# Key tile ahead of the tile of values and gates, in each input quarter of a float32 encoder layer on one core

## The reference

```python
h = rms_norm(x, norm_mix)
proj = h @ w_in      # 2048 x 4624; columns: qa 1024, ka 256, va 256, qf, kf, vf 1024 each, f 16
qa, ka = rope(qa), rope(ka)
out_a = swa_sink_attention(qa, ka, va, sinks)        # 16 query heads, 4 key heads
log_f = log_sigmoid(f_logit + b_f)                   # 16 gates per token
out_b = forgetting_attention(qf, kf, vf, log_f)      # bias: cumulative sum of log_f
x = x + concat(out_a, out_b) @ w_o
h = rms_norm(x, norm_ffn)
x = x + conv_gated_ffn(h, w_up, conv_w, conv_b, w_down)
return rms_norm(x, norm_final)
```

## Time and profile before

| what | kernel before |
|---|---|
| median of 3 runs | 1062.1 us |
| the profiled execution, its own time | 1060.14 us |
| its span, first to last instruction | 1058.3 us |
| PE busy | 1048.7 us (99%) |
| DVE, ACT, POOL busy | 787.5, 626.9, 86.6 us |
| mean DMA rate over the span | 245 GB/s |
| mean granted TensorE clock | 0.998 |

### The profile page before, as it was taken

The page is one execution under the profiler, slowest core; times in us unless marked ns, Lnnn a source line. Parts: engine busy times, 40 slices in busy tenths (PEclk is TensorE's granted clock), DMA queues, the critical chain, the costliest instruction groups (busy, mean ns, idle before and its releaser), DMA issues.

```text
span 1058.3 us, 17826 instructions
## 1 busy us (share of the span) xinstructions
PE 1048.7 (99%) x5945; PEld 904.9 (86%) x5945; DVE 787.5 (74%) x1174; ACT 626.9 (59%) x971; POOL 86.6 (8%) x150
## 2 busy tenths in 40 slices
PE   9999999999999999999999999999999999999997
PEld 8888888888888888888888888888888888888885
DVE  5677677776555777777777877777877888877777
ACT  6956475756455555555655565555656666646663
POOL 1000000011111010111111010101111000000000
PEclk9999999999999999999999999999999999999999
DMA  9575656587888898998898898989889688887993
GB/s 300 173 231 161 186 169 176 168 256 202 246 252 231 263 250 276 253 270 235 256 275 249 267 237 272 268 256 262 249 259 258 224 294 293 274 298 266 322 316 107
DMA packets 191493, 259.35 MB, mean 245 GB/s; under 512 B 10820, under 2 KB 140580, under 8 KB 191328
## 3 DMA queue, kind: packets, MB, share of 16 engines
q1 hardware_dynamic: 173776, 215.32, 63.1%
q0 software_dynamic: 17360, 43.22, 18.7%
q10 hardware_dynamic: 320, 0.34, 0.1%
HBM read 256.73 MB, written 44.06 MB: 284 GB/s over the span
## 4 chain that ended last, share of the span: by engine, by line
PE 98%; DMA 1%; DVE 0%; SPq 0%; ACT 0%; issue 0%; DVEq 0%
PE tr_ps L1579 15%; PE pj L1579 15%; PE pj L1331 9%; PE pj L1581 8%; PE tr_ps L1581 8%; PE pj L1319 5%; PE pj L1320 5%; PE pj L1321 5%; PE pj L1333 5%; PE sc_ps L1319 4%; PE sc_ps L1321 4%; PE sc_ps L1320 4%; PE pj L1346 3%; PE pj L1348 1%; PE tr_ps L1320 1%; PE tr_ps L1321 1%
## 5 line engine op out<-in xcount | busy, mean ns | idle before, releaser
L889 DVE TENSOR_TENSOR split<-raw,split 128x1024 fp32r<-128x1024 f32 x266 | 321.7, 1223 | 146.7 <-ACT split L578 141.4
L578 ACT ACTIVATE split<-raw 128x1024 fp32r<-128x1024 f32 x260 | 270.7, 1057 | 97.2 <-PE pj L1581 28.7
L1579 PE MATMUL tr_ps<-act_split,split 128*128 128x512 f32 x704 | 245.5, 392 | 0.0
L1579 PE MATMUL pj<-act_split,split 128*128 128x512 f32 x704 | 245.0, 391 | 0.0
L1581 PE MATMUL pj<-act_split,split 128*128 128x256 f32 x704 | 197.6, 281 | 0.0
L1581 PE MATMUL tr_ps<-act_split,split 128*128 128x256 f32 x704 | 197.6, 281 | 0.0
L1168 DVE TENSOR_TENSOR split<-raw,split 128x1024 fp32r<-128x1024 f32 (+1 forms) x124 | 137.2, 1136 | 37.9 <-ACT split L834 35.7
L834 ACT ACTIVATE split<-raw 128x1024 fp32r<-128x1024 f32 (+1 forms) x124 | 119.5, 987 | 69.0 <-PE sc_ps L1321 31.9
L1579 PEld LDWEIGHTS tr_ps<-act_split,split 128*128 128x128 f32 x704 | 131.8, 187 | 28.5
L1579 PEld LDWEIGHTS pj<-act_split,split 128*128 128x128 f32 x704 | 131.7, 187 | 28.6
L1331 PE MATMUL pj<-act_split,split 128*128 128x512 f32 x416 | 147.1, 398 | 0.0
(11 more groups left out here) (240 smaller groups left out, 1512.6 us busy)
## 6 DMA issues: line engine op xcount, KB each, us to landing
raw<-w_up SPq DMA_DIRECT2D x176, 512.0 KB, 6.0
raw<-w_in SPq DMA_DIRECT2D x72, 512.0 KB, 3.8
raw<-w_down SPq DMA_DIRECT2D x68, 512.0 KB, 5.6
t_dram<-w_down POOLq DMA_DIRECT2D x60, 512.0 KB, 6.5
raw<-t_dram SPq DMA_DIRECT2D x40, 512.0 KB, 5.7
raw<-w_o SPq DMA_DIRECT2D x32, 512.0 KB, 5.7
t_dram<-t_dram POOLq DMA_DIRECT2D x40, 256.0 KB, 6.0
raw<-w_down SPq DMA_DIRECT2D x20, 256.0 KB, 5.6
```

Of the source, the lines that this page charges most:

```text
L578: ins = act.activation(hi[:, slot, 0:TILE], raw[:, slot, 0:TILE], ACT.Copy)
L889: dve.tensor_tensor(lo[:, slot, 0:n], raw[:, slot, 0:n], hi[:, slot, 0:n].bitcast(F32), ALU.subtract).then_inc(lo_done, 1)
L1579: pe.matmul(up_banks[v][b], wh[:, c, b * P:(b + 1) * P], act_both(k), start=k == 0, stop=False, skip_group_check=True)
```

## The change

In each input quarter the key tile becomes the first of the two (tile 2kt) and the tile of values and gates the second (tile 2kt+1): loads, splits and matmuls change places, the gates' DMA goes out ahead of the values', and `PARTED` becomes `(0, 1)`. The keys accumulate in `pj[:, 0:2]`, values and gates in `pj[:, 2:4]`. The transposes of the next quarter's x move into the middle of `values_and_gates`, ahead of its third chunk. The evacuation of the keys moves ahead on ACT and DVE, and POOL waits for x of quarter 1 before its small loads.

```diff
-PARTED = (0, 2)
+PARTED = (0, 1)
@@ SP
             for kt in range(4):
-                va_slot, ka_slot = 2 * kt % RING, (2 * kt + 1) % RING
+                ka_slot, va_slot = 2 * kt % RING, (2 * kt + 1) % RING
+                load_x(kt)
                 if kt == 0:
-                    load_x(0)
                     sp.dma_start(rows[0:KB, 0], norm_mix...)
                 if 2 * kt >= RING:
                     sp.wait_ge(lo_done, 2 * kt - (RING - 1))
-                sp.dma_start(with_gates(raw, va_slot)[:, :, 0:256], ...)
-                sp.dma_start(with_gates(raw, va_slot)[:, :, 256:VA_COLS], ...)
+                sp.dma_start(narrow(raw, ka_slot), ...)
                 if 2 * kt >= RING:
                     sp.wait_ge(lo_done, 2 * kt + 1 - (RING - 1))
-                sp.dma_start(narrow(raw, ka_slot), ...)
-                if kt < 3:
-                    load_x(kt + 1)
+                sp.dma_start(with_gates(raw, va_slot)[:, :, 256:VA_COLS], ...)
+                sp.dma_start(with_gates(raw, va_slot)[:, :, 0:256], ...)
@@ POOL
             pool.memset(ones[:], 1.0).then_inc(ones_s, 1)
+            pool.wait_ge(d_x[1], 32)
@@ ACT
-            split_hi_early(1)
+            for c in range(4):
+                split_hi_part(1, c)
             for c in range(4, 8):
                 input_hi(c)
-            for c in range(4):
-                split_hi_part(2, c)
+            split_hi_early(2)
             split_hi_early(3)
...
+            act.wait_ge(mm_done, T_QUAD - 1)
+            cross_half(0, rope_a)
             split_hi(T_QUAD, 0)
             act.wait_ge(rms1_done, 1)
-            act.wait_ge(mm_done, T_QUAD - 1)
+            act.wait_ge(mm_done, T_QUAD)
             for m in range(MT):
-                ins = act.activation(va[:, 2 * m], pj[:, m, 0:256], ...)
+                ins = act.activation(va[:, 2 * m], pj[:, 2 + m, 0:256], ...)
...
-            act.wait_ge(mm_done, T_QUAD)
-            cross_half(1, rope_a)
@@ DVE
-            split_lo(1, 1)
+            for c in range(4):
+                split_lo_part(1, c)
             for c in range(4, 8):
                 input_lo(c)
-            for c in range(4):
-                split_lo_part(2, c)
+            split_lo(2, 2)
...
+            join_halves(0, rope_a, 1)
             split_lo(T_QUAD, 0)
...
-            join_halves(1, rope_a, 1)
@@ PE, features: with early=True
+                    if early:
+                        pe.wait_ge(xlo, k + 1)
+                        if t in PARTED:
+                            if c == 3:
+                                pe.wait_ge(lo_done, t + 1)
+                            else:
+                                pe.wait_ge(lo_part, 3 * PARTED.index(t) + c + 1)
@@ PE, values_and_gates
-                t, slot = 2 * kt, 2 * kt % RING
+                t, slot = 2 * kt + 1, (2 * kt + 1) % RING
...
-                    pe.wait_ge(xlo, k + 1)
+                    if c == 2 and kt < 3:
+                        for pr in (2 * kt + 2, 2 * kt + 3):
+                            turn_x_pair(pr)
@@ PE, the first stage
             for kt in range(4):
-                values_and_gates(kt)
-                if kt < 3:
-                    for pr in (2 * kt + 2, 2 * kt + 3):
-                        turn_x_pair(pr)
+                features(2 * kt, 2 * kt % RING, 0, kt, kt == 0, early=True)
                 if kt == 0:
                     pe.wait_ge(cst_c, 1)
-                features(2 * kt + 1, (2 * kt + 1) % RING, 1, kt, kt == 0)
+                values_and_gates(kt)
@@ PE, quad 0
                         if n == 0:
-                                pe.wait_ge(evac_a, 1)
-                                pe.wait_ge(f_abs, 1)
+                                pe.wait_ge(evac_d, 1)
                         if n == 1:
-                                pe.wait_ge(evac_d, 1)
+                                pe.wait_ge(evac_a, 1)
+                                pe.wait_ge(f_abs, 1)
```

More of the change, by code:

```diff
@@ L100, in slot_loads @@
     slot = raw_slot(t)
-    return (T_DOWN // RING * 16 + (32 if slot % 2 == 0 else 0) if slot < RING else 0) + 16 * (len(raw_before(t)) + 1)
+    return (T_DOWN // RING * 16 + (32 if slot % 2 == 1 else 0) if slot < RING else 0) + 16 * (len(raw_before(t)) + 1)
 TSUMS = 2 * len(SUM_KT)
@@ L571, in split_hi @@
             def split_hi(t, slot, paired=False):
-                act.wait_ge(d_w[slot], (t - slot) * (16 // RING) + (48 if slot % 2 == 0 else 16))
+                act.wait_ge(d_w[slot], (t - slot) * (16 // RING) + (48 if slot % 2 == 1 else 16))
                 act.wait_ge(mm_done, t - (RING - 1))
@@ L581, in split_hi_early @@
             def split_hi_early(t):
-                slot, n = t % RING, SLOT if t % 2 == 0 else TILE
-                act.wait_ge(d_w[slot], (t // RING + 1) * (32 if t % 2 == 0 else 16))
+                slot, n = t % RING, SLOT if t % 2 == 1 else TILE
+                act.wait_ge(d_w[slot], (t // RING + 1) * (32 if t % 2 == 1 else 16))
                 if t >= RING:
@@ L589, in split_hi_part @@
             def split_hi_part(t, c):
-                act.wait_ge(d_w[t], 32)
-                ins = act.activation(with_gates(hi, t)[:, c], with_gates(raw, t)[:, c], ACT.Copy)
+                act.wait_ge(d_w[t], 16 if t == 0 else 32)
+                chunks = narrow if t == 0 else with_gates
+                ins = act.activation(chunks(hi, t)[:, c], chunks(raw, t)[:, c], ACT.Copy)
                 ins.then_inc(hi_done if c == 3 else hi_part, 1)
@@ L887, in split_lo @@
                     return
-                n = SLOT if isinstance(t, int) and t < T_QUAD and t % 2 == 0 else TILE
+                n = SLOT if isinstance(t, int) and t < T_QUAD and t % 2 == 1 else TILE
                 dve.tensor_tensor(lo[:, slot, 0:n], raw[:, slot, 0:n], hi[:, slot, 0:n].bitcast(F32),
@@ L897, in split_lo_part @@
                     dve.wait_ge(hi_part, 3 * PARTED.index(t) + c + 1)
-                ins = dve.tensor_tensor(with_gates(lo, t)[:, c], with_gates(raw, t)[:, c], with_gates(hi, t)[:, c].bitcast(F32),
+                chunks = narrow if t == 0 else with_gates
+                ins = dve.tensor_tensor(chunks(lo, t)[:, c], chunks(raw, t)[:, c], chunks(hi, t)[:, c].bitcast(F32),
                                         ALU.subtract)
@@ L1321, in mm3, with features @@
                 return pe.matmul(dst, a_lo, b_hi, start=False, stop=True, skip_group_check=True)
-            def features(t, slot, pair, kt, first):
-                pe.wait_ge(lo_done, t + 1)
+            def features(t, slot, pair, kt, first, early=False):
+                if not (early and t in PARTED):
+                    pe.wait_ge(lo_done, t + 1)
                 wh, wl = narrow(hi, slot), narrow(lo, slot)
```

13 lines of the change are left out of this document (7 added, 6 removed).

## The result

| what | kernel before | changed kernel |
|---|---|---|
| median, from runs side by side on one chip | 1061.96 us (1060.69 to 1063.16, 8 runs) | 1065.47 us (1064.05 to 1067.12, 8 runs) |
| the profiled execution, its own time | 1060.14 us | 1065.49 us |
| its span | 1058.3 us | 1063.7 us |
| PE busy | 1048.7 us | 1051.3 us |

The ratio is 1.0035, with a 95% interval of 1.0026 to 1.0045: the change costs 3.5 us in the median, and 5.35 in the two profiled executions. The forecast was 1064.5 us and +2.4. The ratios of this document leave out three executions of 1303 us at a mean granted clock of 0.752, one of `b1_pool_gates` and two of the kernel before beside it.

The account below looks back on a forecast made before the run. The prediction took PE's work to bound the kernel, so early PE gaps are paid in full. Its terms, -0.4 - 0.25 + 2.25 + 0.8 = +2.4 us on 1062.1, gave 1064.5 us, with 1062.4 to 1067.0 for 8 in 10.

Parts of the forecast that it names:

- What bounds the kernel: Whole span: PE's work sets the time, and a gap of PE in the first 45 us is paid in full.
- The start: Opening: first real matmul 0.4 us sooner, since tile 0 needs no gates' DMA and x lands 0.2 earlier.
- Hitches: First quarter: wait for tile 1 goes as it is split in parts, transposes shorten; net -0.25 us.
- The gap: Second key tile: PE waits 2.25 us for tile 2, split whole behind chunks 4 to 7 of x.
- tile 3 is split during the gap: Second quarter: ACT and DVE split tile 3 while PE stands ahead of tile 2; no size given.
- The gates: Sum of the gates: their pass now comes last, so PE waits at tile 9 and ahead of small matmuls, +0.8 us.
- The clock: PE's gap: the clock falls in it and a stretch runs at half speed, 2.1 us more, 1066.6 us; chance 6%.
- Rival 2: Second key tile and gates: gates' chain covered or first gap only 1.5 us, so +1.6, 1063.7 us; chance 17%.
- Rival 1: Second key tile and gates: no gap, only a faster start, -0.65, 1061.4 us; chance 5%.
- Rival 3: Chunks 12 to 15 of x, tiles 8 and 14: cover breaks, costing 0.5 to 1.5 us, 1065.5 us; chance 14%.
- the range for 8 in 10: Whole kernel: 1062.4 to 1067.0 us, taking in two of the rivals and the spread of the runs.
- the forecast's own range: Whole kernel: 1063.6 to 1065.4 us, by the bounds of the forecast's terms.

Follow-up runs that it names:

- b1_pool_gates: Kernel before, with only POOL's wait for x of quarter 1 and the gates' DMA ahead of the values' added: 1061.08 us, ratio 0.9992.
- b2_before_again: Kernel before, unchanged, profiled a second time to check the pace of PE in the quads: 1061.04 us in one execution.
- a2_changed_again: Changed kernel, unchanged, run and traced a second time: 1064.59 us, ratio 1.0025.
- e6_no_pool_wait: Changed kernel without POOL's wait for x of quarter 1, so its small loads run in the opening: 1067.18 us, ratio 1.0050.
- e4_turn_first: Changed kernel with the next quarter's transposes ahead of the first chunk of the values' pass, not the third: 1062.76 us, ratio 1.0008.
- e1_tile2_ahead: Changed kernel with tile 2 split ahead of chunks 4 to 7 of x on ACT and DVE: 1062.34 us, ratio 1.0008.
- e3_gates_chain: Changed kernel with Exp, Ln and DVE's steps to `nlf_lo` for the gates ahead of the split of tile 10: 1064.77 us, ratio 1.0027.
- e5_both_orders: Changed kernel with tile 2 split ahead of chunks 4 to 7 and the gates' chain ahead of tile 10's split: 1062.33 us, ratio 1.0004.
- e7_busy_gap_8: Changed kernel with 8 small matmuls of ones on PE in the gap ahead of tile 2: 1063.73 us, ratio 1.0020.
- e2_busy_gap: Changed kernel with 15 small matmuls of ones on PE in the gap ahead of tile 2: 1064.51 us, ratio 1.0029.
- e8: Changed kernel with tile 2 split early, the gates' chain ahead of tile 10's split, second square behind chunks 12 to 15: 1062.52 us, ratio 1.0011.
- e9_longer_gap: Changed kernel with two extra copies on ACT ahead of tile 2's split, to lengthen PE's gap: 1067.38 us, ratio 1.0050.

## Why the prediction was right, and where it wasn't

**What bounds the kernel.** It held. Where a delay of PE in the first 45 us was all that differed, it was still there at the end: in `b1_pool_gates` -0.39 and in `b2_before_again` +0.70 at 43 us and at 344 us alike. From 345 to 825 us all the kernels take the same 480.2 us.

**The start, -0.4: -0.24.** Tile 0 comes last in both traces: in the kernel before it lands at 8.20 and ACT takes it up at 8.23, in the changed kernel at 8.00 and 8.02. That is 0.21 of the 0.24, the gain that I had put at 0.1 to 0.2, and the narrower parts are the rest. What failed is the 0.2 for x. It came no earlier (the transposes start at 5.80 against 5.81 in the earlier trace rows), and where its chain is faster the start doesn't move: ACT scales the first chunks at 6.87 in the changed kernel and at 7.09 in `a2_changed_again`, and PE starts at 9.04 and 9.03. Nor was the gates' small DMA all that held tile 0 up, as I had taken it: the key tile is one DMA and still landed only at 8.00. How much POOL's seven loads have in it, one trace without the wait (`e6_no_pool_wait`, 9.02) can't tell from the spread of the others.

**Hitches, -0.25: -0.14.** The work of quarter 0 between the first matmul and the gap takes 4.45 (9.04 to 13.49) + 0.80 + 1.58 = 6.83 us, against 6.97 before (9.28 to 16.25). The transposes came down to 0.80 as forecast. The key tile took 2.94 us and the values 3.09, each 0.08 more than I had read from the rows.

**The gap, +2.25: +2.09.** The chain is 17.96 - 13.49 = 4.47 (forecast 4.55), and PE's own work behind the transposes began 0.80 behind their start and lasted 1.58 (2.38, forecast 2.30). Both lengths are right to 0.1. `e4_turn_first` moves the one and `e1_tile2_ahead` the other, and the gap goes as the sum says. Of the rest of the step, "tile 3 is split during the gap", DVE's row of two tiles, which ends at 19.11, shows that it was done only behind it; nobody waited for it.

**The gates, +0.8: +0.72.** `e3_gates_chain` takes 0.5 of it back. I had put 0.2 ahead of tile 9 and 0.6 ahead of the small matmuls; 0.25 to 0.3 and 0.42 are what PE loses there. The list of waits doesn't show the first, since it is the weight load that waits; it is in all of the new order's traces that were compared (changed, `a2_changed_again`, e1, e3, e5), and is what `e3_gates_chain` keeps.

**Sum up to 43 us.** The terms as measured make -0.24 - 0.14 + 2.09 + 0.72 = +2.43, and `a2_changed_again` is at +2.50, `e7_busy_gap_8` at +2.39. The forecast of +2.4 was that of an execution in which the clock doesn't fall. That it is met to 0.1 is luck in part: the four terms were off by 0.16, 0.11, -0.16 and -0.08, which cancel. Their signs, places and order of size are not luck.

**The clock, a rival at 6%: it came, in some executions.** Here the judgement failed. The forecast had named a fall in either gap as a sign of being wrong, and the profiled execution shows one. I argued from one end of the trace, where 3.2 us of idle time stood before the clock had fallen, that 2.25 are safe; but a fall can come behind the gap too, 1.5 us in the changed kernel and 0.3 in `e6_no_pool_wait`. Of four traces with a gap of 1.93 or 1.94 us two show the fall (the changed kernel, `e6_no_pool_wait`) and two don't (`a2_changed_again`, `e3_gates_chain`). With 3.82 us it fell, and inside the gap. With the array kept busy (`e2_busy_gap`, `e7_busy_gap_8`), with a wait of 1.12 us at most (e1, e4, e5, e8), and in the three traces of the old order it did not. So three of five traces with a gap of 1.93 us or more have the fall, and none of the other nine: that the gap is its condition is well supported, though not what decides between the two outcomes of one kernel. The price that I gave it, 2.1, was 1.6. The time of an execution doesn't tell whether it had the fall: the profiled one of the changed kernel had it and took 1065.49 us, that of `a2_changed_again` had none and took 1065.93, for it lost more later.
The Trainium skill (TensorE: Matmul & The Clock Gate, Part 1) says that an array left idle goes back to half rate until sustained work restores it; `e9_longer_gap` agrees, with 0.50 from inside its gap on, and the changed kernel with 0.50 from 1.5 us behind it.

**Rival 2** (one gap alone) fell: both gaps are there. **Rival 1** (start alone) fell as a forecast, but the direction that it describes is that of `e1_tile2_ahead` and `e5_both_orders`. **Rival 3** (later cover breaks) didn't occur in the changed kernel, tiles 8 and 14 kept their cover; its first place opened in `e5_both_orders`, for 0.9 us, once the gap ahead of it was gone.

**The rest of the median.** The median moved by 3.5, not 2.4: 1.1 more, which is inside the range for 8 in 10 and 0.1 above the forecast's own range. (That range is a little wider than its bounds add up to, 1063.8 to 1065.25.) In `a2_changed_again` the same kernel's median is 2.8 over that of the kernel before (1064.59 against 1061.79), so part of the 1.1 is the spread between sets of runs. Three costs beyond the forecast are seen in the traces and are of the right size. The first is the clock, 1.6 in an execution that has it. The second is the slower pace of the quads, 0.5 for each, which was in no trace of the old order of tiles (three of them) and in eight of the eleven of the new. That doesn't prove that it belongs to the new order: the three old traces are of executions at or below the median of their kernel (1060.14, 1059.75 and 1061.04 us), while of the new ones those with four slow quads lie at or above theirs and those with none below. The third is in the last stage, where PE loses 0.8 us in the changed kernel and 1.8 in e1. There a tile of `w_down` lands late, ACT waits for it, DVE for ACT, and PE for DVE. ACT's row at that tile, in the kernel before, in its repetition and in the changed kernel:

```profile
929.03 1.06 ACT L834 ACTIVATE split<-raw 128x1024 fp32r<-128x1024 f32 x1 [0.22 <-DMA raw<-w_down]
```

```profile
930.32 1.06 ACT L834 ACTIVATE split<-raw 128x1024 fp32r<-128x1024 f32 x1 [1.16 <-DMA raw<-w_down]
```

```profile
934.99 1.06 ACT L834 ACTIVATE split<-raw 128x1024 fp32r<-128x1024 f32 x1 [1.84 <-DMA raw<-w_down]
```

The repetition, with no instruction changed, has it too, and loses 0.2 us by it. Why the tile lands late stays open. How much of the 1.1 each carries in the median can't be told from profiles of single executions. What sets the pace stays open too: no wait and no clock reading goes with it.

**Is there anything to gain?** No: none of these versions is clearly faster than the kernel before. The best of the new order, `e5_both_orders`, is at 1.0004; `b1_pool_gates`, the old order with a faster start, at 0.9992, with no change inside its interval.

## What to carry to other kernels

Here PE turns the input of ACT and DVE in the middle of its own pass, and then needs what they make of it. The gap of PE is the length of their chain, counted from the turning, less the work that PE has left from there; both were read from a trace of the old order to a tenth of a microsecond. Price a new idle stretch of the array with what the clock may take on top, even where a longer stretch elsewhere in the trace shows no fall at once. Where the gap itself can't go, a few matmuls without use in it are worth a try: eight cost nothing here, and the clock held. When a wait is removed, look at the next place in the order that it had been covering. And compare more than one execution of each version before a loss is put down to the change: the moment of the clock's rise, the pace and a late tile each moved single executions by 0.5 to 2 us.

## What the runs showed of the hardware that was not expected

- Behind an idle stretch of 1.93 us of PE the clock falls to 0.50 in some executions (2 of 4) and not in others of the same order of work there. The half pace begins 1.5 us behind the end of the stretch in the changed kernel (19.48) and 0.3 us behind it in `e6_no_pool_wait` (18.27), while PE works, and lasts some 3.4 us, 1.6 us of time lost; with 3.82 us idle it comes inside the stretch and costs 2.4.
- In 2 of 14 traces PE ran at half pace until about 10.3 us (12 rows of the warm-up in 2.69 us, not 1.50), in the others until some moment between 3.8 and 6.5 us. The view's 1.00 ahead of the first record of the clock is no measurement. The late rise cost about 0.7 us.
- Matmuls of 512 and 256 columns in the quads run at 394 and 278 ns or at 400 and 281 ns, for a whole run of tiles at a time, with no wait to show for it: 0.5 us each. Stretches at the slower pace are in traces of both orders.
- A load of 512 KB issued at 2.13 us took 5.87 us to land in the changed kernel. In the other traces of the new order in which ACT stood waiting for it, ACT took it up between 7.84 (`e2_busy_gap`) and 8.22 us (`e3_gates_chain`): the landing moves by 0.4 us between executions with the same opening, more than the change gained at the start.
